# A trunk layer in fp32: bias table stored once and read in reverse query order, gate and attention products reordered by array shape

## The reference

```
x  = LayerNorm(x)
[q|k|v|u|vs|ga|gb] = x @ w_in                      # 1024 x 4608
A  : 8 heads x 64; scores q.k/8 + table[head, clip(key - query, -256, 256)], softmax, @ v
     prompt: a frame reads its own 64-frame chunk and the earlier ones; sample: 256 cached + 64 new frames
B  : gelu(u) * (tril(W_s[g]) @ LN(gelu(vs)) + b_s[g])        # 8 groups x 64 columns, over 128 positions
m  = sigmoid(ga) * (A @ w_branch_a) + sigmoid(gb) * (B @ w_branch_b)
x  = LN1(alpha * x + m @ w_out)
x  = LN2(alpha * x + MoE(x))                       # 64 SwiGLU experts, top-8, and a shared one
x  = x + sigmoid(x @ ple_w_gate) * (p @ ple_w_proj)
```

## Time and profile before

| | us |
|---|---|
| median of 3 runs | 984.96 (981.47 to 986.55) |
| the profiled execution: its own time | 989.87 |
| its span in the trace | 988.1 |
| TensorE busy | 900.7 (91% of the span) |
| VectorE busy | 393.0 |
| ScalarE busy | 258.7 |
| GpSimd busy | 33.6 |
| mean DMA rate | 255 GB/s |

### The profile page before, as it was taken

The page is one execution under the profiler, slowest core; times in us unless marked ns, Lnnn a source line. Parts: engine busy times, 40 slices in busy tenths (PEclk is TensorE's granted clock), DMA queues, the critical chain, the costliest instruction groups (busy, mean ns, idle before and its releaser), DMA issues.

```text
span 988.1 us, 13757 instructions
## 1 busy us (share of the span) xinstructions
PE 900.7 (91%) x4922; PEld 593.1 (60%) x4922; DVE 393.0 (40%) x819; ACT 258.7 (26%) x482; POOL 33.6 (3%) x46
## 2 busy tenths in 40 slices
PE   4609989999989697999999999999999999997987
PEld 4609979965889694444544554455445544552467
DVE  6204357541274666224413432343234323431555
ACT  2104446741143233211221122112211221220342
POOL 3001010000000021000000000000000000000200
PEclk9858999975799888999999999999999999998989
DMA  8658452430178711979999999999999999994201
GB/s 269 96 75 225 130 178 86 162 109 1 43 269 297 297 42 42 393 296 369 411 362 372 370 414 366 370 371 415 362 371 374 412 365 370 374 407 187 101 1 54
DMA packets 81996, 252.16 MB, mean 255 GB/s; under 512 B 7369, under 2 KB 35977, under 8 KB 73522
## 3 DMA queue, kind: packets, MB, share of 16 engines
q1 hardware_dynamic: 77920, 243.39, 65.1%
q0 software_dynamic: 2160, 6.30, 3.9%
q10 hardware_dynamic: 1890, 2.12, 0.7%
HBM read 246.40 MB, written 5.38 MB: 255 GB/s over the span
## 4 chain that ended last, share of the span: by engine, by line
PE 84%; DMA 6%; DVE 5%; issue 1%; ACT 1%; ACTq 1%; SPq 0%; DVEq 0%; PEldq 0%
PE PS L1458 23%; PE PS L1239 20%; PE PS L1473 12%; PE PS L1485 9%; PE PS L1428 9%; DMA weight_ring<-in_w_in_dram 6%; PE PS L1315 1%; PE PS L1314 1%; DVE xs L817 1%; PE PS L1466 1%; DVE xs L827 1%; PE PS L1205 1%; DVE stats L807 1%; PE PS L1445 1%; PE PS L1436 1%
## 5 line engine op out<-in xcount | busy, mean ns | idle before, releaser
L1239 PE MATMUL PS<-parts,split 128*128 128x320 f32 x1536 | 232.3, 313 | 39.2 <-DVE split L853 34.0
L1239 PEld LDWEIGHTS PS<-parts,split 128*128 128x128 f32 x1536 | 229.4, 191 | 41.5 <-DVE split L853 34.5
L1458 PE MATMUL PS<-expert_ring,z 128*64 128x512 f32 x1024 | 230.1, 602 | 6.4 <-issue 6.4
L1458 PEld LDWEIGHTS PS<-expert_ring,z 128*64 128x64 f32 x1024 | 71.3, 138 | 142.9 <-issue 140.7
L853 DVE TENSOR_TENSOR split<-weight_ring,split 128x512 fp32r<-128x512 f32 x106 | 72.8, 697 | 127.0 <-ACT split L583 126.7
L1473 PE MATMUL PS<-expert_ring,z 128*64 128x512 f32 x512 | 116.9, 598 | 0.0
L583 ACT ACTIVATE split<-weight_ring 128x512 fp32r<-128x512 f32 x112 | 69.5, 629 | 148.6 <-PE PS L1239 103.8
L1428 PEld LDWEIGHTS PS<-marks,parts 128*128 128x128 f32 x640 | 80.1, 194 | 31.5 <-issue 31.5
L1485 PE MATMUL PS<-split,marks 128*128 128x512 f32 x384 | 94.2, 399 | 0.3 <-DVE xs L1146 0.3
L1125 DVE SCALAR_TENSOR_TENSOR z<-PS,z 128x256 f32<-128x256 f32 x32 | 15.5, 484 | 196.5 <-ACT z L707 196.5
L1138 DVE TENSOR_TENSOR split<-PS,split 128x512 fp32r<-128x512 f32 x64 | 44.3, 692 | 120.5 <-ACT split L716 120.5
(11 more groups left out here) (205 smaller groups left out, 598.8 us busy)
## 6 DMA issues: line engine op xcount, KB each, us to landing
expert_ring<-in_exp_w_dram SPq DMA_DIRECT2D x256, 512.0 KB, 8.7
expert_ring<-in_exp_w_dram SPq DMA_DIRECT2D x64, 1024.0 KB, 10.4
weight_ring<-in_w_in_dram SPq DMA_DIRECT2D x36, 512.0 KB, 4.4
weight_ring<-in_w_out_dram SPq DMA_DIRECT2D x8, 512.0 KB, 4.5
expert_ring<-in_ple_w_gate_dram SPq DMA_DIRECT2D x2, 2048.0 KB, 9.5
rel_rows<-expert_ring POOLq DMA_DIRECT2D x1, 2308.0 KB, 50.6
weight_ring<-in_w_branch_a_dram SPq DMA_DIRECT2D x4, 512.0 KB, 3.5
weight_ring<-in_w_branch_b_dram SPq DMA_DIRECT2D x4, 512.0 KB, 4.5
```

What stands on the lines that cost most here:

```text
L1239: ins = pe.matmul(out, w[:, wp, :], xT[:, xp, k0 + k, :], start=(start and k == 0 and (wp, xp) == (0, 0)), stop=(stop and k == 3 and wp == 1))
L1458: ins = pe.matmul(PS[c, 2 + j, :], xgT[:, k, P * j + 64 * e:P * j + 64 * e + 64], w13(j, e, k), start=(k == 0), stop=(k == KD - 1))
```

## The change

The table is stored once, as 8 rows of 577 entries. The reads go forward by one entry from partition to partition, so partition r holds the bias of query rows-1-r, and the score tiles are in reverse query order. To match, POOL copies q into qback with the queries of each token tile reversed (after the reads, ahead of the mask of W_s), the scores take qback as the stationary operand, the masks move to the other half of the partitions, and `attend` reads the transposed probabilities with a step of -1. The bias b_s of the gate is no longer a product: it is loaded on all partitions and DVE adds it in two instructions ahead of the multiplication. The products of the gate run token tile by token tile, with the groups (even, odd, even, ...) inside; `turn_probs` does its transposes shape by shape; `attend` alternates the two heads for each product. All loads of ACT's queue but that of the table move to SP, behind the first two chunks of w_in, and the table's load waits for nothing.

```diff
-        bsrow = early(20992, 8, P, rows=1)
+        bs_rows = early(20992, 4, P)
+        mixed = early(23296, 4, TOK)
         lninvec = early(22016, 2, D)
+        qback = early(22016, 4, TOK)
...
-        rel_dram = nc.dram_tensor("rel_rows", (HEADS, P, RW), F32, kind="Internal")
+        rel_dram = nc.dram_tensor("rel_rows", (HEADS, RW), F32, kind="Internal")
...
+        def backwards(a, b):
+            return slice(b - 1, a - 1 if a else None, -1)
...
             for c in range(2):
                 n = slice(c * CH, (c + 1) * CH)
                 load_chunk(c, w_in_v[:, 0:4, n], w_in_v[:, 4:KD, n])
+            sp.dma_start(ck, cache_k[0, 0].rearrange("(a p) h d -> p a (h d)", p=P)).then_inc(cache_loaded, 16)
+            sp.dma_start(ws, mlp_w_s[0].rearrange("g t s -> t g s")).then_inc(ws_loaded, 16)
+            sp.dma_start(cv, cache_v[0, 0].rearrange("(a p) h d -> p a (h d)", p=P)).then_inc(cache_loaded, 16)
+            for i, v in enumerate((mlp_g, mlp_b)):
+                sp.dma_start(mlpvec[:, i, :], v[0].partition_broadcast(P)).then_inc(mlpvec_loaded, 16)
+            for par in range(2):
+                sp.dma_start(bs_rows[64 * par:64 * par + 64, :, :],
+                             mlp_b_s[0, par::2, :].partition_broadcast(64)).then_inc(bs_loaded, 16)
             with sp.Fori(0, CHUNK_STEPS - 1) as i:
                 for c in range(2):
...
             pool.wait_ge(rel_loaded, 16)
             pool.tensor_copy(relpad[:, 0:PAD], relpad[:, PAD:PAD + 1].to_broadcast([HEADS, PAD])).then_inc(rel_padded, 1)
             pool.wait_ge(rel_padded, 1)
-            pool.dma_start(rel_dram.ap(), relpad.unsqueeze(1).to_broadcast([HEADS, P, RW])).then_inc(rel_stored, 16)
+            pool.dma_start(rel_dram.ap(), relpad).then_inc(rel_stored, 16)
             pool.wait_ge(rel_stored, 16)
             def toeplitz(dst, rows, par, keys, first):
-                src = bass.AP(tensor=rel_dram, offset=par * P * RW + first,
-                              ap=[[RW - 1, rows], [2 * P * RW, 4], [1, keys]])
+
+                src = bass.AP(tensor=rel_dram, offset=par * RW + first - (rows - 1), ap=[[1, rows], [2 * RW, 4], [1, keys]])
                 pool.dma_start(dst, src).then_inc(bias_loaded, 16)
             for par in range(2):
@@ -514,6 +528,11 @@
                 toeplitz(prob0[:, 4 * par:4 * par + 4, :], P, par, P, PAD + 256)
                 toeplitz(probs[:, 4 * par:4 * par + 4, :], DH, par, TOK, PAD)
+
+            pool.wait_ge(ln_done, 3)
+            pool.wait_ge(proj_free, 4 + 4)
+            for t in range(3):
+                pool.tensor_copy(qback[:, :, cols(t)], zt[:, Q0:Q0 + 4, backwards(P * t, P * t + ROWS[t])]).then_inc(q_turned, 1)
...
         @block.scalar
         def _(act):
-            act.wait_ge(x_loaded[2], 16)
-            act.dma_start(ck, cache_k[0, 0].rearrange("(a p) h d -> p a (h d)", p=P)).then_inc(cache_loaded, 16)
-            act.dma_start(ws, mlp_w_s[0].rearrange("g t s -> t g s")).then_inc(ws_loaded, 16)
             act.dma_start(relpad[:, PAD:PAD + REL], rel_bias[0]).then_inc(rel_loaded, 16)
-            act.dma_start(cv, cache_v[0, 0].rearrange("(a p) h d -> p a (h d)", p=P)).then_inc(cache_loaded, 16)
-            for i, v in enumerate((mlp_g, mlp_b)):
-                act.dma_start(mlpvec[:, i, :], v[0].partition_broadcast(P)).then_inc(mlpvec_loaded, 16)
-            act.dma_start(bsrow, mlp_b_s[0:1]).then_inc(bs_loaded, 16)
             def norm_std(n):
                 nc.scalar.preload_act_table(ACT.Sqrt)
...
             dve.wait_ge(bias_loaded, 16 * 6)
-            nc.vector.memset(prob1[0:64, :, 192:256], MASKED)
-            after(step(nc.vector.memset(prob0[0:64, :, 64:P], MASKED)))
+            nc.vector.memset(prob1[64:P, :, 192:256], MASKED)
+            after(step(nc.vector.memset(prob0[64:P, :, 64:P], MASKED)))
...
             divide(2)
             dve.wait_ge(mix_ps, 1)
+            dve.wait_ge(bs_loaded, 32)
+            nc.vector.tensor_tensor(mixed[:, :, 0:2 * P].rearrange("p g (t s) -> p g t s", t=2),
+                                    PS[:, 0:4, 0:2 * P].rearrange("p g (t s) -> p g t s", t=2),
+                                    bs_rows.unsqueeze(2).to_broadcast([P, 4, 2, P]), ALU.add)
+            after(step(nc.vector.tensor_tensor(mixed[:, :, 2 * P:TOK], PS[:, 0:4, 2 * P:TOK], bs_rows[:, :, 0:64], ALU.add)))
             dve.wait_ge(gelu_u, 1)
-            nc.vector.tensor_tensor(obT, PS[:, 0:4, 0:TOK], obT, ALU.mult).then_inc(mix_ready, 1)
+            nc.vector.tensor_tensor(obT, mixed, obT, ALU.mult).then_inc(mix_ready, 1)
             dve.wait_ge(ob_high, 1)
             nc.vector.tensor_tensor(xT[:, 1, JW:KD, :], obT, xT[:, 0, JW:KD, :].bitcast(F32), ALU.subtract).then_inc(ob_low, 1)
...
+            pe.wait_ge(q_turned, 3)
             for h in range(HEADS):
                 par, i = h % 2, h // 2
                 ins = pe.matmul(PS[:, 2 * par + i // 2, 256 * (i % 2):256 * (i % 2) + 256],
-                                head(Q0, h, slice(P, 2 * P)), head(K0, h, slice(0, 2 * P)), start=True, stop=True)
+                                query(h, 1), head(K0, h, slice(0, 2 * P)), start=True, stop=True)
             ins.then_inc(score_ps, 1)
...
             pe.wait_ge(ln_done, 6)
-            pe.wait_ge(bs_loaded, 16)
             pe.wait_ge(proj_free, 4 + 4 * CHUNK_STEPS)
-            for g in range(8):
-                par = slice(64 * (g % 2), 64 * (g % 2) + 64)
-                for t in range(3):
-                    n = ROWS[t]
-                    pe.matmul(PS[par, g // 2, cols(t)], ones[0:1, :], bsrow[0:1, g, 0:n], start=True, stop=False)
+            for t in range(3):
+                n = ROWS[t]
+                for g in range(8):
+                    par = slice(64 * (g % 2), 64 * (g % 2) + 64)
                     ins = pe.matmul(PS[par, g // 2, cols(t)], vn[0:n, t, 64 * g:64 * g + 64], wsT[0:n, g, 0:n],
-                                    start=False, stop=True)
+                                    start=True, stop=True)
             ins.then_inc(mix_ps, 1)
...
             def turn_probs(j):
@@ -1323,9 +1342,12 @@
                     pe.transpose(PS[:, b + e, 0:P], prob0[:, h, :], ident[:, :])
                     for c in range(2):
                         pe.transpose(PS[:, b + e, P * (c + 1):P * (c + 2)], prob1[:, h, P * c:P * (c + 1)], ident[:, :])
-                        pe.transpose(PS[:, b + 2, 192 * e + 64 * c:192 * e + 64 * c + 64], probs[:, h, P * c:P * (c + 1)],
+                for e in range(2):
+                    for c in range(2):
+                        pe.transpose(PS[:, b + 2, 192 * e + 64 * c:192 * e + 64 * c + 64], probs[:, 4 * e + j, P * c:P * (c + 1)],
                                      ident[0:DH, 0:DH])
-                    ins = pe.transpose(PS[0:DH, b + 2, 192 * e + 128:192 * e + 192], probs[:, h, 256:TOK], ident[0:DH, 0:DH])
+                for e in range(2):
+                    ins = pe.transpose(PS[0:DH, b + 2, 192 * e + 128:192 * e + 192], probs[:, 4 * e + j, 256:TOK], ident[0:DH, 0:DH])
                 ins.then_inc(probT_ps, 1)
...
             def attend(j):
@@ -1334,16 +1356,23 @@
                 bank = 7 if j % 2 == 0 else 3
                 if j >= 2:
                     pe.wait_ge(oa_ready, j - 1)
-                for e in range(2):
-                    rows, c = slice(64 * e, 64 * e + 64), slice(64 * (2 * j + e), 64 * (2 * j + e) + 64)
-                    pt, ps = probT[:, j, e, :], probT[:, j, 2, :]
-                    pe.matmul(PS[rows, bank, 0:P], v_tok[:, 0, c], pt[:, 0:P], start=True, stop=True)
-                    pe.matmul(PS[rows, bank, P:2 * P], v_tok[:, 0, c], pt[:, P:2 * P], start=True, stop=False)
-                    pe.matmul(PS[rows, bank, P:2 * P], v_tok[:, 1, c], pt[:, 2 * P:3 * P], start=False, stop=True)
-                    o = 192 * e
-                    pe.matmul(PS[rows, bank, 256:TOK], cv[:, 0, c], ps[:, o:o + 64], start=True, stop=False)
-                    pe.matmul(PS[rows, bank, 256:TOK], cv[:, 1, c], ps[:, o + 64:o + 128], start=False, stop=False)
-                    ins = pe.matmul(PS[rows, bank, 256:TOK], v_tok[0:DH, 2, c], ps[0:DH, o + 128:o + 192], start=False, stop=True)
+
+                for product in range(6):
+                    for e in range(2):
+                        rows, c, o = slice(64 * e, 64 * e + 64), slice(64 * (2 * j + e), 64 * (2 * j + e) + 64), 192 * e
+                        pt, ps = probT[:, j, e, :], probT[:, j, 2, :]
+                        if product == 0:
+                            pe.matmul(PS[rows, bank, 0:P], v_tok[:, 0, c], pt[:, backwards(0, P)], start=True, stop=True)
+                        if product == 1:
+                            pe.matmul(PS[rows, bank, P:2 * P], v_tok[:, 0, c], pt[:, backwards(P, 2 * P)], start=True, stop=False)
+                        if product == 2:
+                            pe.matmul(PS[rows, bank, P:2 * P], v_tok[:, 1, c], pt[:, backwards(2 * P, 3 * P)], start=False, stop=True)
```

(6 more changed lines are left out.)

7 lines of the change are left out of this document (5 added, 2 removed).

## The result

The median fell from 984.68 us (981.47 to 986.55) to **908.86 us** (906.02 to 913.1), 4 runs each; the ratio is 0.9254, with a 95% interval of 0.9214 to 0.9294. The forecast was 920, in a range of 905 to 940, and rival 1, at 910, came nearest. The profiled execution took 906.02 us, with a span of 904.0, and is the fastest of its runs, while the one of before (989.87 us) stood above its median; so the two traces differ by 84 us and the medians by 76.

A forecast was written before the change was run, and what follows sets the result against it. TensorE bounded the kernel, idle 33.28 us in stage 1 behind the table's store and slowed by small half-clock products in gate and attention; 35.7 + 3.0 + 26 = 64.7 us saved, giving 920 us, range 905 to 940 (own 914 to 926).

The forecast's parts named there:

- rival 1: From the gate on, TensorE's clock stays up at 2.4 GHz: 36.6 us saved instead of 26, 910 us; chance 0.20.
- The store: Stage 1: without the 128-fold table store ahead of the w_in chunks, TensorE's 33.28 us hole goes; 35.7 us saved.
- the collision: Stage 1: the table's reads meet the first reload of the w_in ring; 0.5 us allowed for it.
- The loads: Ahead of stage 1: loads moved from ACT to SP shorten DVE's waits; 3.0 us saved, bounds 0 and 3.6.
- Copies of q: GpSimd near 40 us: three copies, 2 to 6 us in all, hidden behind stage 1, counted as 0.
- Gate and attention: From the gate to the first branch product on TensorE: 238.9 for 264.60 on the old time axis, 26 us saved.
- The gate: Gate products on TensorE: 5.9 us at the lower clock for 25.4 before; bounds 3.0 and 8.8 us.
- Behind the gate: After the gate, DVE sets the pace for a moment, ahead of `attend(0)`, with TensorE some 1.7 us idle.
- the path of 6.5: DVE from the gate's end to the last copy `attend(0)` needs: 6.5 us for 4.84 before, bounds 6.3 and 7.
- The price of a record: Gate and attend products of 128 columns, alternating halves at the lower clock: 0.145 us each, taken as twice 0.0725.
- the 2.4: Us for one turn of probabilities on TensorE with three changes of shape, for 3.44 before.
- Rival 2: Gate and attend: the halves don't overlap, so 18.4 us saved there and 928 us in all; chance 0.17.

The follow-up runs named there:

- store_128: The changed kernel with the table stored 128 times again (2308 KB from 8 partitions), reads still forward, each partition from its own copy: 943.98 us, ratio 0.9615.
- table_only: The kernel before with only the table stored once, read forward, q copied in reverse and attend reading with a step of -1: 949.44 us, ratio 0.9632.
- loads_on_act: The changed kernel with the loads of caches, W_s, gate vectors and b_s back on ACT's queue: 913.99 us, ratio 0.9326.
- gate_series: The changed kernel with the gate's 8 groups of each token tile run even ones first, then odd ones: 911.69 us, ratio 0.9288.
- attend_by_head: The changed kernel with attend doing all six products of one head, then those of the other: 914.19 us, ratio 0.9338.

## Why the prediction was right, and where it was not

Both main causes that the prediction named were there, and the time lies in its range. It lies outside the 914 to 926 of the forecast proper, though, and that it comes within 1 us of rival 1 is in part luck: two errors that no rival has, 4 us too much in stage 1 and 6 us too little in the tail, nearly cancel.

- **The store.** Right in mechanism and in place: the hole goes with the store alone (store_128, table_only). Sized at 35.7 us saved, it was 31.5 between the traces. The step that was off is the collision, which I allowed 0.5 us. The reload took 15.15 us, not 12.12, and the stop was 2.8; the rest is the clock, 0.92 in the first 15.5 us and 0.62 in the 4 us behind the stop (15.41 + 58.11 us for 71.6). Between the traces of kernels with this stage 1 the idle time is 0.7 to 3.9 us.
- **The loads.** Stage 1 starts 3.1 us earlier, as forecast (3.0); the wait for the standard deviation, 2.38 us, is gone. (I counted eight added issues on SP; they are seven.) But the term isn't simply additive: loads_on_act ends stage 1 only 0.7 us later, within the scatter. I priced start and collision as if they were independent. What the move is worth at the end stays open, between nothing and the 5 us of the medians.
- **Copies of q.** Hidden, as forecast.
- **Gate and attention.** This is the term that was mis-sized most: 26 us saved in the forecast, 36.2 measured. The forecast has 31.1 us from the gate to the branch products (5.9 + 6.5 + 17.2 + 1.5), the trace 20.6. The four attends and two turns account for most of it, 9.4 us (182.90 to 192.31) for 17.2; the gate for 3.3; the waits for DVE took 0.6 more.
- **The gate.** I took half clock but for the first us, as in before, and had 5.9 us; it ran wholly at the full clock in 2.58 (rival 1: 3.0).
- **Behind the gate.** DVE sets the pace, as forecast: from the gate's end at 175.8 to the last copy at 182.75 it is 6.9 us, where 0.55 were the end of the division and 6.4 the path of 6.5. The price of a record, 0.145 us at half clock taken from the rows of 64-row tiles, was too high: an `attend` took 2.3 us at half clock and 1.3 at full, against 3.1 and 1.6. The halves overlap completely there. A turn of 2.30 us at half clock (gate_series, 184.85 to 187.15) bears out the 2.4. At these half-clock durations four attends and two turns would take 13.8 us; so of the 7.8 us that they came out shorter, 3.4 are the price and 4.4 the clock.
- **The clock.** Rival 1 has the gate and the last third; between them lay a stretch at half clock in every trace, some 7 us long in the changed kernel (179.4 to 186.2). The measured 36.2 us is near its 36.6 by luck: a half-clock stretch that it did not foresee, against cheaper products that it did not either.
- **Rival 2** fell with attend_by_head. The rule of "Part 3: Packing small matmuls — row/col tiling" in the Trainium skill's "TensorE: Matmul & The Clock Gate", that weight loads overlap only in another row group, would have made one `attend` 2.6 us, twice the 1.29 of one head; it took 1.30, so in this kernel the trace doesn't agree.
- **The tail.** Nothing in the prediction spoke of the code behind the branch products. Some 4 to 6 us of gain arise there, at the last expert step.
- **The sum.** 64.7 us was forecast and 76 measured. By the traces it is +10 in gate and attention, +6 in the tail and -4 in stage 1, 12 together; the 7.2 us from branch to experts are left out as scatter, and so is how far the two traces stand from their medians.

## What to carry to other kernels

Look at how a small broadcast store is laid out before blaming the ring that stalls beside it: 2.3 MB from 8 partitions took 50.6 us and held a load of 512 KB on another queue for 45 us, and the same bytes took 11.9 us in another form. Order products whose output is half the array's width so that neighbours use different halves, and keep one shape together; at the same clock the first halved `attend`, and taking the one-row products out went with a gate that kept its clock. And a gain at the start of a stage counts only up to the next thing that is late: measure both together.
